# A modulation product moved onto VectorE beside the gate products, and a first expert split during its gather

## The reference

```python
mod = jax.nn.silu(cond) @ w_mod + b_mod            # 2048 -> 6 * 2048, for c and for c_ctx
sh1, sc1, gt1, sh2, sc2, gt2 = jnp.split(mod, 6)
h = rmsnorm(x, g_norm1) * (1 + sc1) + sh1
...   # one input projection; gated linear attention -> o_gla; windowed attention -> o_swa
merged = sigmoid(gate_a) * (o_gla @ w_branch_a) + sigmoid(gate_b) * (o_swa @ w_branch_b)
x = x + gt1 * (merged @ w_out)
h2 = rmsnorm(x, g_norm2) * (1 + sc2) + sh2
x = x + gt2 * expert_choice_ffn(h2, ...)           # 16 SwiGLU experts, each takes its top 64 + 16 tokens
y = rmsnorm(x, g_final)
```

## Time and profile before

| | |
|---|---|
| median of three runs | 2985.25 us (2982.33 to 2985.82) |
| profiled execution | 2982.53 us, span of its trace 2980.7 us |
| TensorE busy | 2837.4 us (95%) |
| VectorE busy | 2062.2 us (69%) |
| ScalarE busy | 1607.4 us (54%) |
| GpSimd busy | 281.0 us (9%) |
| DMA | 684.72 MB, mean 230 GB/s |

### The profile page before, as it was taken

The page is one execution under the profiler, slowest core; times in us unless marked ns, Lnnn a source line. Parts: engine busy times, 40 slices in busy tenths (PEclk is TensorE's granted clock), DMA queues, the critical chain, the costliest instruction groups (busy, mean ns, idle before and its releaser), DMA issues.

```text
span 2980.7 us, 38357 instructions
## 1 busy us (share of the span) xinstructions
PE 2837.4 (95%) x13981; PEld 2100.4 (70%) x13981; DVE 2062.2 (69%) x2384; ACT 1607.4 (54%) x1943; POOL 281.0 (9%) x182
## 2 busy tenths in 40 slices
PE   6899899999999999999999987999999999999993
PEld 4798548899668888888888873666666666666662
DVE  2436655544866766677655556888888888888884
ACT  4345324444854444444343434777777777777773
POOL 0000010000000000000010000111221122111111
PEclk9999999999999999999999998999999999999996
DMA  9822342221023333433362279999999999999994
GB/s 373 291 71 71 123 167 85 76 75 57 1 73 128 132 140 113 157 128 113 137 259 71 84 287 364 401 403 400 383 382 381 389 388 386 378 387 389 388 393 163
DMA packets 160779, 684.72 MB, mean 230 GB/s; under 512 B 13940, under 2 KB 14020, under 8 KB 99004
## 3 DMA queue, kind: packets, MB, share of 16 engines
q1 hardware_dynamic: 147216, 613.45, 53.4%
q0 software_dynamic: 11408, 69.78, 7.4%
q10 hardware_dynamic: 2064, 0.26, 0.1%
HBM read 651.91 MB, written 31.60 MB: 229 GB/s over the span
## 4 chain that ended last, share of the span: by engine, by line
PE 91%; DVE 4%; ACT 2%; DMA 1%; issue 1%; POOL 0%; DVEq 0%; POOLq 0%; ACTq 0%; SPq 0%
PE ps L855 38%; PE ps L1319 24%; PE ps L1346 12%; PE ps L874 5%; PE ps L881 3%; PE ps L1292 1%; PE ps L1146 1%; PE ps L1157 1%; PE ps L819 1%; PE ps L1024 1%; PE ps L1128 1%; PE ps L1256 1%; PE ps L989 1%; DVE ar L1835 0%; PE ps L801 0%
## 5 line engine op out<-in xcount | busy, mean ns | idle before, releaser
L855 PE MATMUL ps<-split_weights,split_tokens 128*128 128x512 f32 x5040 | 1159.0, 391 | 4.4 <-issue 2.9
L855 PEld LDWEIGHTS ps<-split_weights,split_tokens 128*128 128x128 f32 x5040 | 945.2, 188 | 212.8 <-issue 11.5
L1319 PE MATMUL ps<-split_experts,split_xsT 128*80 128x512 f32 x3072 | 709.3, 392 | 4.9 <-DVE split_experts L2074 4.9
L480 DVE TENSOR_TENSOR split_weights<-ring,split_weights 128x512 fp32r<-128x512 f32 x384 | 266.4, 694 | 540.7 <-ACT split_tokens L477 538.6
L476 ACT ACTIVATE split_weights<-ring 128x512 fp32r<-128x512 f32 x384 | 242.7, 632 | 736.8 <-PE ps L855 611.7
L1319 PEld LDWEIGHTS ps<-split_experts,split_xsT 128*80 128x80 f32 x3072 | 454.9, 148 | 257.4 <-DVE split_experts L2074 5.8
L2074 DVE TENSOR_TENSOR split_experts<-hT,split_experts 128x2048 fp32r<-128x2048 f32 x240 | 548.0, 2289 | 75.6 <-ACT split_experts L1657 75.4
L1657 ACT ACTIVATE split_experts<-hT 128x2048 fp32r<-128x2048 f32 x240 | 460.7, 1920 | 153.2 <-PE ps L1319 111.8
L1346 PE MATMUL ps<-split_experts,split_hidT 128*80 128x512 f32 x1536 | 361.0, 394 | 0.0
L1346 PEld LDWEIGHTS ps<-split_experts,split_hidT 128*80 128x80 f32 x1536 | 225.5, 148 | 121.9
L483 DVE TENSOR_TENSOR split_tokens<-hT,split_tokens 128x640 fp32r<-128x640 f32 x304 | 250.5, 824 | 0.0
(11 more groups left out here) (261 smaller groups left out, 1929.0 us busy)
## 6 DMA issues: line engine op xcount, KB each, us to landing
ring<-w_mod SPq DMA_DIRECT2D x96, 1024.0 KB, 5.3
hT<-w_exp_gate SPq DMA_DIRECT2D x80, 1024.0 KB, 7.2
hT<-w_exp_up SPq DMA_DIRECT2D x80, 1024.0 KB, 7.1
hT<-w_exp_down SPq DMA_DIRECT2D x80, 1024.0 KB, 9.5
ring<-w_in SPq DMA_DIRECT2D x64, 1024.0 KB, 5.2
ring<-w_exp_gate SPq DMA_DIRECT2D x32, 1024.0 KB, 8.0
ring<-w_exp_up SPq DMA_DIRECT2D x32, 1024.0 KB, 10.3
ring<-w_exp_down SPq DMA_DIRECT2D x32, 1024.0 KB, 7.6
```

What stands on the lines that cost most here:

```text
L480: a = self.eng.tensor_tensor(spW[:, s, 1, :], raw, spW[:, s, 0, :].bitcast(F32), ALU.subtract)
L855: mm = pe.matmul(ps[:, b, :], spX[:, s, x, b * P:(b + 1) * P], spW[:, s, w, :], start=(k == 0 and x == w), stop=(k == n_k - 1 and x == 1))
L1319: mm = pe.matmul(ps[0:CAP, bank + i, :], xsT[:, x, k, :], spE[:, s, w, col:col + BANK], start=(k == 0 and x == w), stop=(k == KT - 1 and x ...
```

## The change

Part 5 of the modulation joins parts 3 and 4 beside the gate products. Each turn now loads 24 granules, strictly one for a product and one of `w_mod`, and has 48 modulation rows in three pairs of accumulators. `MOD_ROWS` puts them on pieces 3 to 23 and 27 to 47: 24 rows on 21 pieces, so pieces 3, 10, 17, 27, 34 and 41 have two. TensorE's sums come at pieces 20 and 37 of the turn, and the third one at piece 6 of the next turn (the last at piece 7 of the output product). The TensorE granules of part 5 with their loads are gone. SyncE's queue loads two expert granules into ring slots as soon as the output product's granules are used up, and five after the norm. ScalarE splits the first three granules before it waits for the gathered tokens, behind the stores of `x1` and `h2`, whose buffers the splits reuse; VectorE makes their low parts right behind the top-k copies, before the tokens' low parts. The load of `w_router` and the buffer for `g_norm2` move.

```diff
@@ -65,19 +65,17 @@
-G_OUT = G_GATE + 4 * 20
-G_M4 = G_OUT + 4 * 4
-G_M_PART = [G_M2, G_M4]
+G_OUT = G_GATE + 4 * 24
-    return 5 * (j // 3) + 2 * (j % 3)
+    return 2 * j
-    return 5 * (m // 2) + 1 + 2 * (m % 2)
+    return 2 * m + 1
@@ -98,6 +96,7 @@
+MOD_ROWS = [[r for r in range(48) if 3 + 24 * (r // 24) + r % 24 * 21 // 24 == k] for k in range(48)]
...
@@ -289,8 +288,9 @@
-        mod_acc = cst[:, P:P + 4 * BANK].rearrange("p (j w n) -> p j w n", j=2, w=2)
-        mod_ones = cst[:, P + 4 * BANK:P + 4 * BANK + 32]
+        mod_acc = [cst[:, P + BANK * i:P + BANK * (i + 1)] for i in range(5)] + [area(29776, BANK)]
+        mod_ones = cst[:, P + 5 * BANK:P + 5 * BANK + 32]
+        g2_half = area(12800, BANK)
@@ -306,7 +306,7 @@
-        exp_slot = [hT_area(i * SLOT, SLOT) for i in range(5)] + [area(25344, SLOT), ring[:, 0, :], ring[:, 1, :]]
+        exp_slot = [ring[:, 0, :], ring[:, 1, :]] + [hT_area(i * SLOT, SLOT) for i in range(5)] + [area(25344, SLOT)]
...
@@ -372,28 +372,27 @@
-                j, kk = (first + k) // 4, (first + k) % 4
-                if j % 3 == 2:
-                    return
-                dve, m = sp.eng, 2 * (j // 3) + j % 3
-                half, row, g = m // 4, 4 * (m % 4) + kk, G_GATE + mod_place(m)
-                v = ring[:, g % SLOTS, kk * BANK:(kk + 1) * BANK]
-                if kk == 0:
-                    dve.wait_ge(slot_ready[g % SLOTS], n * 80 + 16 * (g // SLOTS + 1))
-                if row == 0:
-                    dve.wait_ge(s_mT, n * 2 + (half + 7))
-                for who in range(2):
-                    acc, c = mod_acc[:, half, who, :], cond32[:, row, who:who + 1]
+                dve = sp.eng
+                for r in MOD_ROWS[first + k]:
+                    m, kk = r // 4, r % 4
+                    part, row, g = m // 4, r % KT, G_GATE + mod_place(m)
+                    v = ring[:, g % SLOTS, kk * BANK:(kk + 1) * BANK]
+                    if kk == 0:
+                        dve.wait_ge(slot_ready[g % SLOTS], n * 96 + 16 * (g // SLOTS + 1))
-                        dve.tensor_scalar(acc, v, c, None, ALU.mult).then_inc(z_rd, 1)
-                    else:
-                        dve.wait_ge(z_rd, n * 64 + (2 * GH + 32 * half + 2 * row + who))
-                        dve.scalar_tensor_tensor(acc, v, c, acc, ALU.mult, ALU.add).then_inc(z_rd, 1)
-                if kk == 3:
-                    dve.wait_ge(z_rd, n * 64 + (2 * GH + 32 * half + 2 * row + 3))
-                    dve.sem_inc(slot_used, 1)
-            sp.pieces(P_GATE + first, n * 48, lambda k: G_GATE + gate_place((first + k) // 4), n * 5,
+                        dve.wait_ge(s_mT, n * 3 + (part + 6))
+                    for who in range(2):
+                        acc, c = mod_acc[2 * part + who], cond32[:, row, who:who + 1]
+                        if row == 0:
+                            dve.tensor_scalar(acc, v, c, None, ALU.mult).then_inc(z_rd, 1)
+                        else:
+                            dve.wait_ge(z_rd, n * 96 + (2 * GH + 32 * part + 2 * row + who))
+                            dve.scalar_tensor_tensor(acc, v, c, acc, ALU.mult, ALU.add).then_inc(z_rd, 1)
+                    if kk == 3:
+                        dve.wait_ge(z_rd, n * 96 + (2 * GH + 32 * part + 2 * row + 3))
+                        dve.sem_inc(slot_used, 1)
+            sp.pieces(P_GATE + first, n * 48, lambda k: G_GATE + gate_place((first + k) // 4), n * 6,
@@ -565,18 +564,12 @@
-                    load((G_GATE + gate_place(j), n * 20), src, k4)
-                    if j % 3 < 2:
-                        m = 2 * (j // 3) + j % 3
-                        cols = ds(n * (2 * BANK) + (3 * D + m // 4 * BANK), BANK)
-                        load((G_GATE + mod_place(m), n * 20), w_mod[:, 4 * (m % 4):4 * (m % 4) + 4, cols], k4)
+                    load((G_GATE + gate_place(j), n * 24), src, k4)
+                    cols = ds(n * BANK + 5 * D, BANK) if j >= 8 else ds(n * (2 * BANK) + (3 * D + j // 4 * BANK), BANK)
+                    load((G_GATE + mod_place(j), n * 24), w_mod[:, 4 * (j % 4):4 * (j % 4) + 4, cols], k4)
-            def last_modulation(lo, hi):
-                for j in range(lo, hi):
-                    load((G_M4 + j, 0), w_mod[:, j, 5 * D:6 * D])
@@ -589,19 +582,19 @@
-            last_modulation(0, 7)
+            sync.wait_ge(slot_used, SLOTS + G_OUT + 16)
+            for j in range(2):
+                expert(0, j)
-            for j in range(5):
+            for j in range(2, 7):
-            last_modulation(7, KT)
-            sync.wait_ge(slot_used, SLOTS + G_M4 + 16)
-                for j in range(5, EXP_G):
+                for j in range(7, EXP_G):
-                for j in range(5):
+                for j in range(7):
-            for j in range(5, EXP_G):
+            for j in range(7, EXP_G):
...
@@ -664,17 +653,17 @@
-            pool.wait_ge(pv_pe, len(units))
-            pool.dma_start(wrt, T["w_router"][0].rearrange("(k p) e -> p k e", p=P)).then_inc(wr_ld, 16)
-            def mod_sum(n, half):
-                pool.wait_ge(mc_ev, 2 * n + half + 2)
-                cols = slice(3 * D + (2 * n + half) * BANK, 3 * D + (2 * n + half + 1) * BANK)
+            def mod_sum(n, part):
+                pool.wait_ge(mc_ev, 3 * n + part + 2)
+                at = 5 * D + n * BANK if part == 2 else 3 * D + (2 * n + part) * BANK
+                cols = slice(at, at + BANK)
+                    mod_sum(n - 1, 2)
...
@@ -735,11 +725,10 @@
-            mod_part(5, 10)
-            pool.wait_ge(mc_st, 64 + 16 * 8 + 64)
+            pool.wait_ge(mc_st, 64 + 16 * 12)
-            pool.wait_ge(slot_used, SLOTS + G_M4 + 16)
+            pool.wait_ge(slot_used, SLOTS + G_OUT + 16)
...
@@ -1178,25 +1167,24 @@
-            def merged_transpose(n, b):
+            def merged_transpose(n, b, sums):
-                    pe.wait_ge(mc_ev, n * 2 + 3)
+                    pe.wait_ge(mc_ev, sums)
-            def mod_sum(n, half, before):
-                pe.wait_ge(z_rd, n * 64 + (2 * GH + 1 + 32 * (half + 1)))
-                if before is not None:
-                    pe.wait_ge(mt_cp, n * NT + (NT - 1 - NT))
-                if half or before is not None:
-                    pe.wait_ge(mc_ev, n * 2 + (1 + half))
+            def mod_sum(n, part, bank_copied=None):
+                pe.wait_ge(z_rd, n * 96 + (2 * GH + 1 + 32 * (part + 1)))
+                if bank_copied is not None:
+                    pe.wait_ge(mt_cp, bank_copied)
+                pe.wait_ge(mc_ev, n * 3 + (1 + part))
-                    mm = pe.matmul(ps[32 * who:32 * who + 32, 7, :], mod_ones, mod_acc[:, half, who, :],
+                    mm = pe.matmul(ps[32 * who:32 * who + 32, 7, :], mod_ones, mod_acc[2 * part + who],
@@ -1212,13 +1200,17 @@
-                        if first + k in (22, 46):
-                            mod_sum(n, (first + k) // 24, before)
+                        if first + k == 6 and before is not None:
+                            mod_sum(before, 2)
+                        if first + k == 20:
+                            mod_sum(n, 0, None if before is None else n * NT + (NT - 1 - NT))
+                        if first + k == 37:
+                            mod_sum(n, 1)
-                            merged_transpose(before, b)
+                            merged_transpose(before, b, n * 3 + 1)
@@ -1229,7 +1221,9 @@
-                    merged_transpose(3, k - 1)
+                    merged_transpose(3, k - 1, 12)
+                if k == NT + 2:
+                    mod_sum(3, 2, 4 * NT - 1)
@@ -1239,7 +1233,6 @@
-            mod_granules(3)
@@ -1280,7 +1273,6 @@
-            mod_granules(7)
@@ -1300,13 +1292,10 @@
-            mod_granules(3)
-            mod_granules(3)
-            pe.wait_ge(mc_ev, 10)
@@ -1384,18 +1373,15 @@
-            def mod_part(i):
-                act.wait_ge(slot_used, SLOTS + G_M_PART[i] + KT)
-                if i:
-                    act.wait_ge(mc_st, 64 + 16 * 8)
-                    act.wait_ge(g2_f, 1)
-                act.activation(modc[:, :], ps[:, 7 - i, :], ACT.Copy).then_inc(mc_ev, 1)
-            def mod_sum(n, half):
-                act.wait_ge(s_mT, n * 2 + (9 + half))
-                act.wait_ge(mc_st, n * 32 + (64 + 16 * half))
+            def mod_part():
+                act.wait_ge(slot_used, SLOTS + G_M2 + KT)
+                act.activation(modc[:, :], ps[:, 7, :], ACT.Copy).then_inc(mc_ev, 1)
+            def mod_sum(n, part):
+                act.wait_ge(s_mT, n * 3 + (9 + part))
+                act.wait_ge(mc_st, n * 48 + (64 + 16 * part))
...
@@ -1575,7 +1561,12 @@
-                gate_split(sp, n, 0, AHEAD, KT)
+                if first:
+                    gate_split(sp, n, 0, AHEAD, KT)
+                else:
+                    gate_split(sp, n, 0, AHEAD, 14)
+                    mod_sum(n - 1, 2)
+                    gate_split(sp, n, 0, 14, KT)
@@ -1585,7 +1576,10 @@
-                    gate_split(sp, n, q + 1, AHEAD, 8)
```

(17 more changed lines are left out.)

32 lines of the change are left out of this document (15 added, 17 removed).

## The result

| | before | after |
|---|---|---|
| median | 2985.36 us (2981.76 to 2989.77, 10 runs) | 2993.97 us (2987.08 to 2996.57, 10 runs) |
| profiled execution | 2982.53 us, span 2980.7 | 2992.71 us, span 2990.9 |

The ratio is 1.0029, 95% interval 1.0019 to 1.0039: 8.6 us slower. The forecast was 2990 within 2981 to 2997. The time lies in the range. Beside the prediction's bound of 0.2% it reads as slower, which had a chance of 0.32, though the interval's low end (0.19%) lies just inside that bound; the likeliest value was 4 us too low. The end of the trace comes 10.2 us later than before; the trace is read against that number. It compares one profiled execution of each kernel, so terms of some tenths can belong to the execution.

A forecast was written before the change was run, and what follows sets the result against it. The prediction took TensorE, 91% of the last-ending chain, as the bound; 4.9 - 0.5 - 0.8 + 1.1 - 5.4 + 4.8 + 0.1 + 0.5 = +4.7 us gave a median of 2990 us, range 2981 to 2997.

The forecast's parts named there:

- step 6: First expert's start: -5.4 us for work leaving the chain, +4.8 for gathered rows landing later, +0.1 for transposes.
- Steps 1 and 2: Gate stage and output product: more modulation on VectorE costs 0; four more sums on TensorE cost 4 x 1.23 = +4.9 us.
- Step 3: Borders in the gate stage: evictions start sooner without rows, -0.7 us; the last border loses its cover, +0.2; together -0.5.
- Step 4: Tail of the attention: two modulation operations leave the chain before the last softmax, -0.8 us, or -0.4 at half clock.
- Step 5: Stretch before the norm: an extra expert granule ahead delays GpSimd's four row loads, +1.1 us, bounds 0 and 2.5.
- step 7: TensorE's clock in the first expert: half clock lasts a little longer after longer idling, +0.5 us, between -0.5 and +1.5.
- landing at 1826.1, +4.8: First expert: gathered rows land later through held copy, longer gather instruction and loads; +4.8 us, bounds 0 and 6.5.
- The gather lands as in a running expert: Rival at the first expert: gather lands 10.2 us from issue, sum +6.4 or more, 2992; chance 0.24.
- GpSimd isn't held: Rival at the first expert: the gather goes as before, the start keeps its 5.4, sum about 0, 2985; chance 0.14.
- VectorE becomes the bound: Rival in the gate stage: pieces with two modulation rows each stall TensorE, +14 on the +4.7, 3004; chance 0.05.
- A gain of over 6 us: Rival for the whole kernel: every bound at its best gives only -3.9, so something unseen is needed; chance 0.07.

The follow-up runs named there:

- the merged sum: The changed kernel with the third part's sum of a turn made together with the first part's sum of the next; 2990.27 us, ratio 1.0018.
- the narrow sum: The changed kernel with TensorE's sums of the third modulation part over 32 of 512 columns; 2989.79 us, ratio 1.0018.
- the run with pauses: The changed kernel with VectorE waiting for the end of each of its three early splits before the next; 2992.68 us, ratio 1.0027.
- the run with both edits: The changed kernel with VectorE's early splits behind the gather's issue and SyncE's late granules behind its landing; 2985.26 us, ratio 0.9998.

## Why the prediction came out as it did

| step | predicted, us | in the trace, us | where |
|---|---|---|---|
| 1 to 3, gate stage and output product | +4.4 | +4.7 | shift at 852: 0.08, at 1589: 4.82 |
| 4, tail of the attention | -0.8 | -0.3 | shift at 823: 0.39, at 852: 0.08 |
| 5, row loads | +1.1 | +0.3 | shift at the norm: 5.10 |
| norm to the index copy | 0 | -0.7 (clock) | 4.38 at the copy |
| 6, first expert's start | -0.5 | +5.7 | 10.04 at its first matmul |
| 7, clock | +0.5 | +0.3 | 46.12 against 45.86 |

With the 0.39 that was there before the tail, and 0.1 less behind the start of the last expert, that is the 10.2 of the profiled execution. The median moved by 8.6; 4.7 was forecast. The range held because its upper end, 2997, had room for step 6 going wrong, not because the landing of the rows was foreseen.

*Steps 1 and 2 were right.* VectorE's 128 operations more cost nothing, and a stop for a sum costs 1.23 us: measured by the merged sum (1.22 a turn) and by one row with the sums at the borders (1.21), and the narrow sum takes 0.85 of it away.

*Step 3 had the right size for a wrong reason, which is luck.* Both of its prices are 0.06 and 0.07 us too low: 54.74 - 54.43 is 0.31 and not 0.24, so a border of before costs 0.41 and not 0.34; and the output product's border costs 0.24 in the block of the earlier trace rows only, 0.30 in the next (`54.73 PE ps L855 x240`). The difference, 0.10 a border, is the one forecast, and the measured one: a turn is 1.03 us longer, 1.23 less two times 0.10. But the prediction took the border of before as the price of a row ahead of it. That row costs 1.3 us when no sum stands ahead, and the sum, not the lighter rows, is what takes the last 0.3 off. The step's size held because the change moved both.

*Step 4* was too large by half a microsecond: with the modulation operations gone, ScalarE's splits of the same pieces are next on the chain there (`849.63 0.63 ACT split_tokens L476`). *Step 5* was too large as well: the loads landed 0.28 us late, not 1.1 (from the output product's last block to the norm the twelve kernels of the experiments take 0 to 0.45 us more than the 60.31 of before). Neither can be told from nothing in a median. The 0.7 us up to the copy was not in the sum, and the change didn't win it: it is one group of 16 router matmuls, `1762.53 2.63 PE ps L1256 x16` before and `1.91` after. In the first microsecond of that group the granted clock was 0.50 before and 0.89 after. In the other kernels, whose programs are the same there, the group takes 1.85 to 2.48 us. So a part of the profiled difference belongs to the execution and not to the kernel; with step 7's +0.3 it is -0.5 us.

*Step 6 failed in one term*, "landing at 1826.1, +4.8"; it measured +10.9. It had three parts: about 2 us for a copy held by one split, 1.6 to 1.8 for the longer gather instruction, 1 for the loads. From the copy's start to the first transpose of the rows took 6.37 us before and 17.28 after, +10.9. The copy was held 6.4 us, because these splits follow each other with no pause: the earlier trace rows show a copy that ends 0.04 us behind the split it met, and in the same rows a pause of 0.32 us follows, which the prediction did not look for in the place where the three splits would stand. The instruction was not held at all (0.98 us), since no split was left. The gather took 4.5 us longer from its issue, for four loads were issued just ahead of it, three of them within 4.5 us, where before the nearest had left 6.5 us ahead and the DMA engines' share was down to 0.13 (1815 to 1817 us); with the four gone it took 4.9 less. Putting the gather ahead of the splits, and so of most loads, wins 6.2 us, taking the loads away 4.9, both 9.3 and not 11.1, since a gather issued first is itself held beside the splits. The other parts of step 6 were right: from the landing to the product 5.63 us where 5.5 was forecast, and without hold and loads the start keeps 3.6 of its 5.4.

The Trainium skill's rule ("SBUF — State Buffer", Who interferes with whom), that the port pair which VectorE shares with GpSimd is an exclusive lock and the second instruction is blocked for the whole of the first, gives the 2.18 us of the run with pauses. It says nothing of three in a row; by 6.58 us the copy isn't let in between instructions that follow without a pause. The same section infers that descriptor generation isn't held. The gather's instruction seems to say otherwise, 2.95 us beside the splits and 0.98 without, and the prediction took the earlier trace rows as evidence against the inference. But GpSimd's plain loads agree with it. Two of them in the kernel before, issued beside two splits with no pause between these, take 0.60 and 0.54 us, and 0.55 with VectorE elsewhere:

```profile
1838.16 1.14 POOL L615 DMA_DIRECT2D ar<-mod_rows  x2 [6.48 <-DMA mod_rows<-modc]
```

The gather also has to read its 80 indices from SBUF. Whether that read is what is held was not tried.

*The rivals.* "The gather lands as in a running expert" came nearest: 10.38 us against its 10.2, and later for the hold ahead of it. Its price, 2992, was short of the hold by the second and third split. "GpSimd isn't held" has 2985, and the run with both edits gave 2985.3; the mechanism is not the same, since the gather's instruction is still held there and the start wins 3.6 us and not 5.4. "VectorE becomes the bound" is not what happened, but the run with one row beside each piece (3003.6 against its 3004) has that time for another reason: the doubles that the rival feared are harmless, and the rows ahead of the evictions do it. That the two numbers agree is chance. *A gain of over 6 us* was argued from the best bounds, whose sum is -3.7 and not -3.9; it changes nothing.

What stays open: why the half clock lasts 3.0 us in one first expert and 6.1 in another, what part of the gather's instruction is held, and which part of the gather's time beside loads is waiting in its queue and which is slower transfer.

## What to carry to other kernels

Before work is moved into an idle stretch of one engine, look at what a second engine has to start there with a tiny instruction, and put the issue of that first: a 0.18 us copy in front of a gather became 6.58 us, and each slot that the moved work frees can send a megabyte ahead of the transfer that everybody waits for. A stop of one engine can be the cover of another's lateness: when a small interruption is moved, price what stood in its shadow, here 1.3 us a border, and put unavoidable stops just where another engine is late. And interruptions whose matmuls can run side by side, here on different partitions of a bank, cost as one when they stand in one place.

## What the chip showed that was not expected

- A GpSimd copy of 80 words was held through three VectorE operations of 2.28 us that followed each other without a pause (6.58 us), and through one of them (2.18 us) when VectorE waited for the end of each before the next. Between the two cases lie 0.11 us: splits that overlap by 0.08 in the records, and splits 0.03 apart.
- The gather's instruction beside such operations took 2.95 or 2.85 us against 0.98, and ended within the split that follows the one it began in, not behind the last. Plain loads of GpSimd's took 0.54 to 0.60 us beside such operations, as without them.
- Loads of 1 MB from SyncE's queue delayed a gather of GpSimd's by when they were issued. With its instruction not held it landed 5.48 us from its issue with no load near, 5.86 with two that left behind its instruction, 7.62 with one 0.13 us ahead and 10.38 with four ahead. With the instruction held it was 7.47 with none, 10.56 with one ahead and three behind its start, 12.54 with two ahead and two behind.
- Eight matmuls of a sum, on four groups of 32 partitions, interrupt the product for as long as four on two: 1.00 us against 0.98. With 32 columns for 512 the four took 0.18.
- The same 192 matmuls of a first expert took 45.63 to 47.11 us with no wait in them; what differed was how long the granted clock stayed at half.
